# Two blocks on one core: the norms behind both MLPs by halves of the tokens, with their sums partly on TensorE

## The reference

```
def _rmsnorm(x, g):
    y = x * lax.rsqrt(jnp.mean(x * x, axis=-1, keepdims=True) + NORM_EPS)
    return y * g

def first_block(x, params):
...
    hid = jnp.square(jax.nn.relu(m @ w_mlp_in))
    h = h + hid @ w_mlp_out
    return _rmsnorm(h, norm_final_g)           # gain g_fin

def second_block(x, params):
    h = rms_norm(x, ln1_g)                     # gain g_ln1
    z = h @ w_in + b_in                        # q, k, v and more
...
    x = x + jnp.square(jax.nn.relu(h2 @ w_ff1)) @ w_ff2
    return rms_norm(x, lnf_g)                  # gain g_lnf
```

## Time and profile before

| what | us |
|---|---|
| three runs | 2910.07, 2916.06, 2910.53; median 2910.53 |
| the profiled execution | 2909.63 |
| its span | 2907.8 |
| TensorE busy | 2858.7 (98%) |
| VectorE busy | 1692.7 (58%) |
| ScalarE busy | 1320.1 (45%) |
| mean granted TensorE clock | 0.994 |

### The profile page before, as it was taken

How to read it: one execution, slowest core, us unless ns; L and a number is a source line. 1 busy time by engine, 2 the same in 40 slices (tenths; PEclk the granted TensorE clock), 3 DMA queues, 4 the chain that set the end, 5 groups by cost and what they waited for, 6 DMA issues and landing times.

```text
span 2907.8 us, 34459 instructions
## 1 busy us (share of the span) xinstructions
PE 2858.7 (98%) x13080; PEld 2272.0 (78%) x13080; DVE 1692.7 (58%) x2411; ACT 1320.1 (45%) x2120; POOL 188.1 (6%) x136
## 2 busy tenths in 40 slices
PE   8999999999999999999999999999999999999997
PEld 6777777888888878887677787777888888878885
DVE  4333355235866666687555524888235866666785
ACT  4444452114655554454355424777124645544452
POOL 1222410000000000000222100000000000000000
PEclk9999999999999999999999999999999999999998
DMA  3111111123333475541311111211113334384441
GB/s 123 37 37 37 37 37 51 51 62 127 131 149 145 158 275 191 156 127 55 132 51 52 37 58 52 63 53 44 58 57 139 131 146 158 130 320 154 153 134 58
DMA packets 84971, 302.71 MB, mean 104 GB/s; under 512 B 9424, under 2 KB 9552, under 8 KB 78544
## 3 DMA queue, kind: packets, MB, share of 16 engines
q1 hardware_dynamic: 83088, 294.31, 29.7%
q10 hardware_dynamic: 1728, 6.29, 0.7%
HBM read 225.07 MB, written 75.50 MB: 103 GB/s over the span
## 4 chain that ended last, share of the span: by engine, by line
PE 55%; issue 43%; DVE 2%; ACT 0%; POOL 0%; DMA 0%; POOLq 0%; DVEq 0%; SPq 0%; ACTq 0%
PE ps L2243 16%; PE ps L371 9%; PE ps L2512 5%; PE pa L2512 5%; PE ps L2541 5%; PE pa L2541 5%; PE ps L2388 2%; PE pa L2315 2%; PE pa L2287 2%; PE ps L2557 2%; PE pa L2296 1%; PE pa L2260 1%; PE pa L2388 0%; PE pa L2202 0%; DVE res L1408 0%
## 5 line engine op out<-in xcount | busy, mean ns | idle before, releaser
L361 DVE TENSOR_TENSOR w_lo<-w_raw,w_hi 128x1024 fp32r<-128x1024 f32 x134 | 159.5, 1191 | 445.6 <-ACT w_hi L355 445.5
L355 ACT ACTIVATE w_hi<-w_raw 128x1024 fp32r<-128x1024 f32 x134 | 137.8, 1029 | 414.2 <-PE ps L371 276.7
L371 PE MATMUL ps<-a_hi,w_hi 128*128 128x512 f32 x896 | 281.8, 396 | 0.3 <-DVE a_lo L1607 0.3
L371 PE MATMUL ps<-a_hi,w_lo 128*128 128x512 f32 x896 | 280.9, 395 | 0.0
L371 PE MATMUL ps<-a_lo,w_hi 128*128 128x512 f32 x896 | 280.8, 394 | 0.0
L2243 PE MATMUL ps<-a_hi,w_hi 128*128 128x512 f32 x704 | 236.6, 417 | 12.2 <-DVE a_lo L1555 8.8
L1140 ACT ACTIVATE krh<-k_rraw 128x512 fp32r<-128x512 f32 x192 | 121.0, 630 | 235.6 <-PE ps L2541 117.2
L2243 PE MATMUL ps<-a_lo,w_hi 128*128 128x512 f32 x704 | 225.8, 402 | 0.0
L2243 PE MATMUL ps<-a_hi,w_lo 128*128 128x512 f32 x704 | 225.6, 401 | 0.0
L1841 DVE TENSOR_TENSOR krl<-k_rraw,krh 128x512 fp32r<-128x512 f32 x192 | 132.5, 690 | 135.1 <-ACT krh L1140 134.8
L371 PEld LDWEIGHTS ps<-a_hi,w_hi 128*128 128x128 f32 x896 | 167.8, 188 | 43.4 <-issue 2.5
(11 more groups left out here) (322 smaller groups left out, 5943.4 us busy)
## 6 DMA issues: line engine op xcount, KB each, us to landing
w_raw<-wstream SPq DMA_DIRECT2D x134, 512.0 KB, 3.5
k_rraw<-hff SPq DMA_DIRECT2D x224, 256.0 KB, 2.7
hff<-hbuf SPq DMA_DIRECT2D x32, 1024.0 KB, 3.9
wA<-wff SPq DMA_DIRECT2D x16, 2048.0 KB, 8.1
hff<-hbuf SPq DMA_DIRECT2D x32, 768.0 KB, 3.3
w_raw<-wff SPq DMA_DIRECT2D x32, 512.0 KB, 4.2
f_raw<-wff SPq DMA_DIRECT2D x32, 512.0 KB, 4.4
hres<-zt SPq DMA_DIRECT2D x16, 512.0 KB, 2.6
```

Of the source, the lines that this page charges most:

```text
L355: nc.scalar.activation(w_hi[:, slot, 0:n], w_raw[:, slot, 0:n], ACT.Copy).then_inc(s_whi, 1)
L361: nc.vector.tensor_tensor(w_lo[:, slot, 0:n], w_raw[:, slot, 0:n], w_hi[:, slot, 0:n].bitcast(F32), ALU.subtract).then_inc(s_wlo, 1)
L371: mm = nc.tensor.matmul(out[0:m, c], w[0:kp, slot, wofs:wofs + m], x[0:kp, k, c * HC:(c + 1) * HC], start=first and n == 0, stop=last and ...
```

## The change

- The plain and the scaled square are no longer taken both by ScalarE: tiles 4 to 7 are squared whole and added by VectorE (`end_sum`, which weights the square by g_fin squared for `sqsum_g`). Tiles 0 to 3 are squared by halves into `sqh` and never added: TensorE sums them. `one2` holds for each tile the pair (1, g_fin squared) of each channel as the input of these matmuls, so that one matmul gives both sums.
- `end_stats(b, 0, 0)` sums the first token half ahead of part 5 of the product, its broadcast comes inside part 6, `end_stats(b, 1, 0)` inside part 7; the rest of the second half's sum, tile 3 alone (`end_stats(b, 1, 1)`), follows the product.
- Behind MLP 1 five half tiles of the first half are normed under the product. `first_units` on TensorE takes units 0 and 1 together, first token half, then second; the residual's broadcast comes between the ends of the two units, and VectorE scales the residual there. GpSimd no longer makes any `a_lo`.
- Behind MLP 2 the first half is scaled and stored under the product, the second behind it, in half tiles.
- SP waits for the eight stores to land and then issues the bias loads that ScalarE's queue had, ahead of the mask and the weights of unit 4.
- A11 and A12 (two blocks of MLP weights) and `r6l` exchange places in memory.

```diff
@@ sync
             for k in range(KT):
                 sp.wait_ge(sem("s_nrm"), k + 1)
                 sp.dma_start(x2[k * P:(k + 1) * P], res[:, k]).then_inc(sem("s_stored"), 16)
-            sp.wait_ge(sem("s_nlo"), KT // 2)
-            sp.wait_ge(sem("s_nle"), KT // 2)
+            sp.wait_ge(sem("s_stored"), 16 * KT)
+            for o in range(3):
+                sp.dma_start(braw[:, 2 * o:2 * o + 2], bias2[0, :, 2 * o:2 * o + 2]).then_inc(sem(f"s_braw{o}"), 16)
+            sp.wait_ge(sem("s_nle"), 2 * KT)
+            sp.wait_ge(sem("s_ebc"), 3)
             sp.dma_start(msk[:], mask2).then_inc(sem("s_cst"), 16)
             units(STAGES["att2"].u + 4, STAGES["out2"].u + 2)
@@ vector, mlp(b)
+                end_sum(1)
                 l6_lo(5)
+                end_sum(2)
+                end_sum(3)
                 c12(0)
...
+                l6_lo(7)
+                end_mean(b, 0, 0)
                 c12(1)
+                end_diag(b, 0)
                 c12(2)
+                if b == 1:
+                    norm_tile(0)
...
+                    norm_lo(4)
+                else:
+                    scale_half(0)
+                end_mean(b, 1, 0)
                 c12(3)
@@ tensor
+            def end_stats(b, c, part):
+                n = 2 if b == 1 else 1
+                out = pa[:, c, 8 * part:8 * part + 8]
+                tiles_ = (3,) if part else range(3) if c else range(4)
...
+                for i in range(4):
+                    blk = slice(i * P, (i + 1) * P)
+                    if not part:
+                        for a, src in enumerate((sqsum, sqsum_g)[0:n]):
+                            nc.tensor.matmul(out[:, 2 * i:2 * i + n], src[:, c * HC + i * P:c * HC + (i + 1) * P],
+                                             one2[:, 8 + a] if b == 1 else ones[:, 0:1], start=a == 0, stop=False)
+                    for m in tiles_:
+                        mm = nc.tensor.matmul(out[:, 2 * i:2 * i + n], sqh[:, m, blk],
+                                              one2[:, m] if b == 1 else ones[:, 0:1],
+                                              start=bool(part), stop=m == tiles_[-1])
...
+                    for idx in range(KT + 4):
+                        if idx == KT:
+                            pe.wait_ge(sem("s_fin"), KT)
+                        pe.wait_ge(sem("s_nle"), idx + 1)
+                        for m in range(2):
+                            part(m, idx)
+                        if idx == 1:
+                            end_stats(1, 1, 1)
+                        if idx == 4:
+                            end_broadcast(1, 1)
...
                 for j in range(N6):
...
+                    if j == 5:
+                        end_stats(b, 0, 0)
                     for kk in range(8):
                         k = 8 * hf + kk
+                        if (j, kk) == (6, 2):
+                            end_broadcast(b, 0)
+                        if (j, kk) == (7, 4):
+                            end_stats(b, 1, 0)
```

More of the change, by code:

```diff
@@ L76 @@
 U_ATT2, U_GAT0, U_GATT, U_REC, U_MRG2 = 3 * N_PAIR2 + EXTRA + 1, 3, 6, 25, 15
-SPREADS = (1, 2, 4, 5, 6)
+SPREADS = (1, 2, 3)
+NORM_ORDER = [(k, c) for c in range(2) for k in (4, 5, 6, 7, 2, 3, 0, 1)]
+EARLY = 5
 NPAIR = 16
@@ L537, in _ @@
             mlp(2)
[L538 to L541, removed]
+            for c in range(2):
+                for k in range(KT):
+                    sp.wait_ge(sem("s_nrm"), KT * (c + 1) + k + 1)
+                    sp.dma_start(outT[k * P:(k + 1) * P, half(c)], res[:, k, half(c)]).then_inc(sem("s_stored"), 16)
+            sp.wait_ge(sem("s_stored"), 48 * KT)
         def tile_of(idx):
@@ L661, in _ @@
                     windows(p)
-            norm_power(1, rstd, msg)
-            norm_power(2, rstd1, ms)
-            norm_lo()
+            for c in range(2):
+                end_power(1, c)
             pool.wait_ge(sem("s_cst"), 32)
@@ L679, in _ @@
                                         ALU.add).then_inc(sem("s_bm"), 1)
-            norm_power(3)
+            for c in range(2):
+                end_power(2, c)
         @block.scalar
@@ L699, in copy_rb, with norm_hi @@
                                      ).then_inc(sem("s_rb"), 1)
[L701 to L704, removed]
+            def norm_hi(idx):
+                k, c = NORM_ORDER[idx]
+                act.wait_ge(sem("s_nd"), idx + 1)
+                act.wait_ge(sem("s_l6lo"), N6)
+                nc.scalar.activation(a_hi[:, k, half(c)], normed(idx), ACT.Copy).then_inc(sem("s_nh"), 1)
             def attention(b):
@@ L1217, in mlp @@
                 l6_hi(4)
[L1218 to L1221, removed]
+                for item in range(3):
+                    end_square(item)
+                l6_hi(5)
+                end_square(3)
                 if b == 1:
@@ new lines, in residual, with scale_half @@
+            def residual(k):
+                dve.wait_ge(sem("s_ebc"), 3)
+                nc.vector.scalar_tensor_tensor(out=res[:, k], in0=res[:, k], scalar=V("g_fin", k),
+                                               in1=pa[:, 0:2].rearrange("p c n -> p (c n)"),
+                                               op0=ALU.mult, op1=ALU.mult).then_inc(sem("s_nrm"), 1)
+            def scale_half(c):
+                dve.wait_ge(sem("s_ebc"), 3 + c + 1)
+                for k in range(KT):
+                    nc.vector.scalar_tensor_tensor(out=res[:, k, half(c)], in0=res[:, k, half(c)],
+                                                   scalar=V("g_lnf", k), in1=pa[:, 2 + c],
@@ L1491, in attention @@
                 for m in range(AHEAD):
+                    if b == 2 and m == 0:
+                        residual(0)
                     weights(m)
+                    if b == 2 and m == 0:
+                        for k in range(1, KT):
+                            residual(k)
                     if b == 1 and m == 0:
@@ L2648, in _ @@
             mlp(2)
-            stats(4)
-            broadcast(5)
+            end_stats(2, 1, 1)
+            end_broadcast(2, 1)
 def tiles(w, n, width=P, rows=P):
```

316 lines of the change are left out of this document (194 added, 122 removed).

## The result

| | before | change |
|---|---|---|
| median, us | 2916.06 (2910.07 to 2922.04, 13 runs) | 2923.25 (2917.57 to 2930.46, 13 runs) |
| profiled execution, us | 2909.63 | 2919.51 |
| its span, us | 2907.8 | 2917.7 |

The ratio is 1.0026, with a 95% interval of 1.0014 to 1.0037: the change makes the kernel slower by about 7.5 us. In a second series it was 1.0028 (1.0019 to 1.0038): 2920.35 against 2912.82. The three runs known ahead of the prediction were on the fast side of the kernel before (2910.53 against 2916.06 over all runs), so the difference is smaller than the distance from that number.

A forecast was written before the change was run, and what follows sets the result against it. TensorE, busy 2858.7 of 2907.8 us, bounds the kernel. Seam +8.4 and end +2.4 give +10.8 us: 2909.6 becomes 2920.4 for the profiled execution, 2921 for the median, range 2907 to 2926.

The forecast's parts named there:

- Seam, TensorE's own work, -10.6: Between MLP 1 and block 2's second unit: TensorE's work takes 37.3 us against 47.9, saving 10.6 us if nobody is late.
- VectorE and ScalarE in time: At the seam: squares and half tiles are ready before TensorE asks for them, so they cost nothing.
- The queue, +10.6: SP's queue at the seam: the fifth unit's weights land at about 1428, TensorE stands still 10 us, +10.6 us (+7 to +12).
- Its clock, +2.2: After TensorE's idle ten microseconds at the seam: the clock falls, 3.3 to 5.5 us at half cost +2.2 us.
- The clock in the sums, +6.2 and +4.4: In both blocks' bursts of sums: they count as rest, the clock falls; block 1 +6.2 us, block 2 +4.4 us.
- End, -2.9 + 0.9: At the kernel's end: sums add 9.2 us, the tail saves 12.1, leaving -2.9; its broadcast at half clock costs +0.9.
- The sum: Whole kernel: seam +8.4 and end +2.4, together +10.8 us on the profiled execution, 2920.4.
- Rival 1: Bursts of sums: the clock holds because TensorE is never idle, the queue's stall stays; +0.2 us, 2910.7; chance 0.30.
- Rival 3: At the seam: weights land before the third unit ends, no stall, clock holds; -12.6 us, 2897.9; chance 0.13.

The follow-up runs named there:

- The kernel with both edits: The change with unit-5 and unit-6 weight loads issued before the wait for the stores, and sums spread in small parts: 2899.90 us, 0.996 of before.
- experiment 1: The change with only SP's queue reordered, fifth and sixth units' weight loads ahead of the wait for the stores: 2910.68 us, 0.999 of before.
- the idle sums: The kernel before plus 192 unread single-column matmuls in its last products: bursts of 24 2984.51 us, parts of 6 2957.72, bursts of 12 2984.40, against 2912.32.
- the change again: The changed kernel run once more, nothing altered, for a second trace: 2920.35 us, 1.0028 of before.
- experiments 4 and 5: The kernel before with 192 unread matmuls: 2984.51, 2957.72, 2984.40 us; the change with queue reordered, sums spread, block 2's sums behind its product: 2908.88 us.

## Why the prediction was right

The forecast (2921, slower as the likeliest) came out, and by the mechanisms it named, though the nearness of 2921 to 2923.25 is partly luck. Step by step:

- **Seam, TensorE's own work, -10.6.** The kernel with both edits shows it alone: 105.6 against 115.8 and 114.6, so -10.2 or -9.0. Right.
- **VectorE and ScalarE in time.** TensorE waits for no square and no tile at the seam. Right. Eight scalings of the residual end at 1417.0; I had 1414.4.
- **The queue, +10.6.** A stall of 10.18 us; weights issued at 1422.4 and landed at 1430.9, where I had 1428. It was late by 3 us because the stores began later and the landing took 8.5 us. TensorE was later at that point too, so the stall came out at 10 all the same. Right in place, mechanism and size; experiment 1 takes it away by order alone.
- **Its clock, +2.2.** 10.2 us at half in both traces, most of it during the stall; what lies behind it is 2.8 us in the first (1433.6 to 1436.4) and 3.8 in the second, so 1.4 and 1.9.
- **The clock in the sums, +6.2 and +4.4.** The mechanism is right: the clock falls at such a burst though TensorE has no pause, and the idle sums show it with nothing else in the way, at 3.3 us for a burst of 24. In detail the fall comes 2.5 to 5.3 us after the start of a burst rather than 3.6, sometimes just behind its end, and then lasts 3.4 us or a multiple. (The row at half clock that the prediction took it from has 16 matmuls in 32 records, not 32 matmuls; the reading is the same.) Block 1 cost 3.4 us in the first trace (two falls behind the bursts) and 6.8 in the second; block 2 1.7 and 3.4. So these two terms are each over by one or two microseconds.
- **End, -2.9 + 0.9.** -3.2 in the kernel with both edits, where no fall comes ahead of the tail. Right within about a microsecond; the last broadcast ran at half clock (2.07 us), as assumed.
- **The sum**, +10.8 on the profiled execution: the traces give +5.4, the runs +7.5. Against the runs it is over by 3 us, which the two clock terms above cover on average (5.1 and 2.6 against 6.2 and 4.4). Against the two measures of the traces it is over by 5: the end also came out a microsecond better. The 2.1 us between traces and runs are not accounted for; a fall behind the pause of the earlier trace rows and the slow pace could be in them. The absolute 2921 was met because the three runs it stood on lay 2 to 5 us below the longer series.

Rival 1, the clock that holds in the sums, rested on TensorE not being idle. The Trainium skill (TensorE: Matmul & The Clock Gate, section Why this matters for your kernels) asks for no long idle gaps between bursts of matmuls; by that rule these sums would be free. No gap was there, and the idle sums cost 26.8 us beyond their length: the rule as it stands is not enough here, and the measurement decides. Rival 3, both going well, is what experiment 3 built: I had 2897.9 for it, and 2899.9 was measured.

## What to carry to other kernels

When small work is moved onto the engine that bounds a kernel, look at what it does to the clock: here narrow fp32 matmuls in one parcel of 12 or 24 cost 1.7 or 3.3 us beyond their length, the same in parcels of 6 with 6 wide ones between almost nothing beyond it (+45 us against +43 for 32 of them). When loads are moved to another queue, write down what stands behind each new wait on it; here two loads of weights, moved ahead of the wait for the stores, were worth 10 us. And a traded gain can be right in every part and still lose: the gain of 12 us was real, and it took two small repairs, both in the order of instructions, with one added wait, to keep it.

## What was not expected of the hardware

- **The clock falls at bursts of 2.6 us.** 12 narrow matmuls between 12 wide ones brought the clock down to 1.2 GHz at each of the eight bursts of block 1, for 3.4 us each time; a true pause of 3.2 to 3.4 us did so in seven traces of twelve.
- **The same fall has several lengths.** At the same first burst the clock stood at half for 3.4, 6.8 and 10.2 us in three traces that share that code (the change, the queue kernel, the change again).
- **Two paces at full clock.** The products of an MLP ahead of its last run at 439 or at 430 matmuls in 100 us, for the whole of that stage (4.7 us longer), in 4 of 24 cases, all in kernels built on the change. The granted clock on record for every run says how far the falls go: in the 13 runs of the change it was 0.993 for the fastest (2917.57 us) and 0.990 for the slowest (2930.46), which is an estimated 9 of the 13 us between them. It doesn't cover everything: span times granted clock, an estimate of the time at full clock good to 1.5 us, still runs from 2887 to 2897 us over the 13 runs of the kernel before that were taken beside experiments 4 and 5. Whether the slow pace is in those runs can't be seen without their traces. All this is why one trace can't be compared with another by its span alone.
